# Placing every SBUF tile, and the arena, at a multiple of 256 bytes instead of 128

## The reference

```python
for l in range(DEPTH):                      # DEPTH = 2
    m = silu(c) @ ada_w[l] + ada_b[l]       # shifts, scales and gates
    h = modulate(x, m[0], m[1])
    if l % 2 == 0: y = even_mixer(h, hc, ...)      # SSD scan and HGRN2 scan, with a context of 256 tokens
    else:          y = conformer_conv(h, ...)      # gated product, depthwise conv of 31 taps, product
    x = layer_norm(ALPHA * x + m[2] * y)
    x = layer_norm(ALPHA * x + m[5] * conv_glu_ffn(modulate(x, m[3], m[4])))

def conv_glu_ffn(t, w_up, conv_w, conv_b, w_down, rows, cols):
    v, gate = jnp.split(t @ w_up, 2, axis=-1)      # 1024 -> 2 x 2816
    gate = dwconv2d(gate, conv_w, conv_b, rows, cols)
    return (gelu(gate) * v) @ w_down               # 2816 -> 1024
```

## Time and profile before

| | us |
|---|---|
| median of 3 runs | 2833.45 |
| lowest, highest run | 2827.32, 2833.52 |
| profiled execution, its own time | 2828.01 |
| its span, first to last instruction | 2826.2 |
| PE busy (16080 matmuls) | 2643.6 |
| VectorE busy | 1644.6 |
| ScalarE busy | 1090.9 |
| GpSimd busy | 161.7 |

### The profile page before, as it was taken

One profiled execution on the slowest core, in us unless ns is written; L12 is line 12 of the kernel. 1 busy time (PEld: TensorE's weight loads), 2 busy tenths in 40 slices (PEclk: granted clock), 3 DMA queues, 4 the chain that ended last, 5 costly groups with the idle time before them and its releaser, 6 DMA issues. The chain is left out here.

```text
span 2826.2 us, 41654 instructions
## 1 busy us (share of the span) xinstructions
PE 2643.6 (94%) x16080; PEld 2040.3 (72%) x16080; DVE 1644.6 (58%) x2595; ACT 1090.9 (39%) x1805; POOL 161.7 (6%) x170
## 2 busy tenths in 40 slices
PE   6978899988889999999998999999899998999998
PEld 3753598876668788887664788888588765788876
DVE  3526412257766587853898688853763676544432
ACT  3441211136563455521524455522321254355421
POOL 0005300013213000000000000000000000000000
PEclk9989999999999999999999999999999998999999
DMA  8734312211114133241111233331431000233241
GB/s 306 246 108 145 124 46 60 59 43 40 43 44 131 46 109 91 87 123 47 55 49 34 68 107 94 96 113 52 124 91 45 3 17 28 86 96 96 82 119 61
DMA packets 382116, 240.93 MB, mean 85 GB/s; under 512 B 7825, under 2 KB 353809, under 8 KB 381969
## 3 DMA queue, kind: packets, MB, share of 16 engines
q1 hardware_dynamic: 381968, 238.89, 28.1%
HBM read 236.24 MB, written 2.10 MB: 84 GB/s over the span
## 5 line engine op out<-in xcount | busy, mean ns | idle before, releaser
L1164 DVE SCALAR_TENSOR_TENSOR ffn_acc<-ffn_pad,cols_sb,ffn_acc 128x512 f32<-128x512 f32 x380 | 263.6, 745 | 31.2 <-ACT ffn_acc L1091 31.1
L249 PE MATMUL bank<-ffn_x_high,pre_high 128*128 128x512 f32 x528 | 209.4, 397 | 4.9 <-DVE ffn_x_low L480 3.8
L251 PE MATMUL bank<-ffn_x_high,pre_low 128*128 128x512 f32 x528 | 207.3, 393 | 0.0
L250 PE MATMUL bank<-ffn_x_low,pre_high 128*128 128x512 f32 x528 | 207.3, 393 | 0.0
L251 PE MATMUL bank<-ffn_x_high,ffn_w_low 128*128 128x512 f32 x528 | 205.5, 389 | 0.0
L249 PE MATMUL bank<-ffn_x_high,ffn_w_high 128*128 128x512 f32 x528 | 205.5, 389 | 0.0
L250 PE MATMUL bank<-ffn_x_low,ffn_w_high 128*128 128x512 f32 x528 | 205.4, 389 | 0.0
L249 PE MATMUL bank<-ffn_h_high,ffn_down_w_high 128*128 128x512 f32 x480 | 188.7, 393 | 0.0
L251 PE MATMUL bank<-ffn_h_high,ffn_down_w_low 128*128 128x512 f32 x480 | 187.7, 391 | 0.0
L250 PE MATMUL bank<-ffn_h_low,ffn_down_w_high 128*128 128x512 f32 x480 | 187.6, 391 | 0.0
L754 ACT ACTIVATE ffn_down_w_high<-ffn_down_ring 128x1408 fp32r<-128x1408 f32 (+1 forms) x45 | 60.5, 1344 | 207.1 <-PE bank L251 175.7
(11 more groups left out here) (732 smaller groups left out, 6237.8 us busy)
## 6 DMA issues: line engine op xcount, KB each, us to landing
ada_ring<-in_ada_w SPq DMA_DIRECT2D x48, 1024.0 KB, 7.0
pre_ring<-in_ffn_w_up SPq DMA_DIRECT2D x88, 512.0 KB, 3.7
pre_ring<-in_ffn_w_in SPq DMA_DIRECT2D x44, 512.0 KB, 3.7
ffn_down_ring<-in_ffn_w_down SPq DMA_DIRECT2D x28, 704.0 KB, 4.5
pj_ring<-in_w_in SPq DMA_DIRECT2D x24, 512.0 KB, 3.5
ffn_down_ring<-in_ffn_w_out SPq DMA_DIRECT2D x14, 704.0 KB, 4.4
pre_ring<-in_conf_w SPq DMA_DIRECT2D x18, 512.0 KB, 4.8
f_ring<-in_mix_w_in SPq DMA_DIRECT2D x32, 256.0 KB, 3.2
```

The costliest lines, as they stand in the source:

```text
L249: pe.matmul(bank, weights[0], acts[0], start=start, stop=False)
L250: pe.matmul(bank, weights[0], acts[1], start=False, stop=False)
L251: return pe.matmul(bank, weights[1], acts[0], start=False, stop=stop)
L1164: dve.scalar_tensor_tensor(out=dst, in0=src, scalar=conv_w(2 * i + j, n), in1=dst, op0=ALU.mult, op1=ALU.add).then_inc(tapped[j], 1)
```

## The change

One constant, that every request for a place in SBUF names:

```diff
 ARENA = 28 * 1024
-LINE = 128
+LINE = 256
```

## The result

The changed kernel takes 2812.76 us (median of 6 runs, 2804.01 to 2816.26) against 2830.97 us for the kernel before (6 runs, 2827.32 to 2833.52). The ratio is 0.9933, with a 95% interval of 0.9916 to 0.9950: faster by 14 to 24 us. The forecast was 2818 us, in a range of 2811 to 2827. The profiled execution took 2811.28 us.

The account below looks back on a forecast made before the run. TensorE was taken as the bound in the feed-forward loops, by matmul count times start distance, 5.6 ns dearer for pairs 128 apart. Eight terms summed to 12.8 us; 2830.6 less that gave 2818 us, range 2811 to 2827.

Parts of the forecast that it names:

- Terms 1 to 3: Gains: gate slabs of ffn0 and ffn1 5.4 us; ffn2's down product 2.7; first 16 arena blocks of three down products 0.8.
- Terms 4 and 8: Projections from `pj_w`: 2.1 us gained at 512 tokens, and 0.4 (between 0 and 1.1) where they stream 384 columns.
- Term 5: First projection, `xbc_w`: 288 matmuls no longer 128 apart, 1.1 us gained, between 0 and 1.6.
- Term 6: The second block's first 16 output blocks from the arena: 48 matmuls, 0.3 us gained.
- Term 7: Conformer: 192 matmuls and 48 in its output product, between 0 and 1.3 us; taken as 0, under VectorE's taps.
- VectorE and loads at nothing: Slab splits change at most 8 ns, under PE's work, and ring landing times stay alike; both counted as 0.
- Nothing happens: Rival: distance between starts hangs on something else about the arena, such as its height; 2828 to 2833 us, chance 0.07.
- Half lost: Rival: PE gives time back in other waits, items 3 to 6 go; 2823 to 2827 us, chance 0.14.
- Cheaper loads: Rival: arena loads landing at multiples of 256 get cheaper, some 9 us more at 38 to 170 us; 2809, chance 0.03.
- 256 apart costs: Rival: about 1820 more matmuls 256 apart modulo 512, ffn0's and ffn1's down products first, cost too; up to 2840, chance 0.03.

## Why the prediction was right, and where not

**Cause.** Weights and activations that stand 128 apart modulo 256 cost, in products of 512 and of 384 columns; the place of neither does. Shown from both sides: the arena at 128 is slow by activations at 0 and fast by activations at 128, and the kernel with everything at 128 is as fast as the changed one. The Trainium skill, "SBUF — State Buffer", section "Who interferes with whom", calls TensorE's two read ports independent; the 226.7 against 232.4 ns of these runs speak against it for this pair of reads. What happens inside the chip when the two stand apart, these runs don't show; they show the price by distance.

**Terms 1 to 3** (5.4 + 2.7 + 0.8). The loops gave 2.9 us each and ffn2's down product with its first blocks 2.9, where 2.7, 2.7 and 3.0 stood. The first 48 matmuls of a loop gave nothing, as forecast: in ffn0 they take 14.01 us before (961.88 to 975.89) and 14.00 after (964.88 to 978.88), paced by the activations. The loops' 0.2 us over the forecast lie in the ten later arena blocks, 11.16 to 10.88 us or 5.8 ns a matmul, and in the stack's, 10.89 to 10.88. The first blocks of ffn0 and ffn1 went from 232.6 to 227.7 ns, 0.2 us each; the down products behind them scatter by up to 1 us from trace to trace, so in the whole stretch that doesn't show.

**Terms 4 and 8** (2.1 + 0.4), and **what the sum lacked**. Without the clock's part, the projections gave 5.9 less 3 to 3.5, or 2.4 to 2.9 us, and the pitch of the products of 384 columns went from 178.1 to 175.6 ns, 0.5 us: both terms hold. What failed is the step that a time saved before a stage's waits can only be lost in them; the sum has no term for the clock, which it put at nothing without a reason. With the quicker products, 3 to 3.5 us that half clock had cost in the projections went, and 2.0 to 3.6 us in attention. That, 5 to 7 us, is about what lies between the sum of 12.8 and the gain, 18.2 us by the medians and 20.4 by the ratio of the repeated runs; the gain's interval, 14 to 24 us, is too wide to check it more closely.

**Term 5** (1.1, between 0 and 1.6). The pitch of `xbc_w` went from 232.4 to 227.6 ns, but the stage's time scatters by 2 us and more with its half clock (203.1 before, 205.7 and 201.3 after), so what arrived can't be read. Beside it the same weights go over the context's tokens in 240 matmuls of 256 columns, also 128 apart before, which the count left out. They gave nothing: their pitch is 122.1 to 122.4 ns in the four traces with that distance and 123.1 in the eight with 0. **Term 6**: 233.1 to 227.3 ns and 52.5 to 52.2 us, the 0.3 forecast. **Term 7**: the pitch of the conformer's arena products fell from 232.4 to 228.2 ns and the stage stayed at 196.3 to 196.5, under VectorE's taps, as argued from the earlier trace rows.

**VectorE and loads at nothing**: medians of 1220 and 1225 ns after against 1219 and 1225, and landings at most 0.2 us shorter; both hold, since the gain comes without the shorter landings too, with every tile 128 off.

**The rivals.** Nothing happens: refuted by the pitches. Half lost: nothing came back as waits in the loops, since PE has none there but the first activations. Cheaper loads: refuted by the kernel with every tile 128 off, whose loads land in 4.5 and 4.4 us and whose time is the changed kernel's; and the modulation's weights, which the rival went by, land in 7.0 to 7.4 us before and 7.1 to 7.4 after. The argument against it was too strong, though: the earlier trace rows compared two stages, and within one, ffn2, a ring 128 off costs 4.4 us against 4.2. The Trainium skill, "DMA: Bandwidth & Descriptors", section "How a descriptor splits into AXI transactions", says that a descriptor that doesn't start at a multiple of 256 bytes costs extra beats; these 0.2 us agree with it in direction. 256 apart costs: ffn0's down product reads 226.7 ns at that distance.

**The number.** 2818 was 5 us too high, about the clock's part; the range held it by 1.8 us at its low end. That end came from every term at its full price and the lowest base, rounded down, and not from anything that could give more, so that it held is in part luck: 2 of the 6 runs lie below it.

## What to carry to other kernels

Where TensorE is the bound and takes one pass of 512 columns after another (at 256 columns nothing was to be gained here), place the weight tile and the streamed tile alike modulo 256 bytes (both at 0, or both at 128), and look for the mismatch in the distance between starts, since the duration of a matmul shows 4 ns of the 5.6. Price such an edit per pair, by the matmuls that stand apart before and after: it is worth 2.4% of their time, and a careless shift of one tile can cost as much. In a stage with short pauses of TensorE, trace the kernel before more than once before a few microseconds are put down to an edit or to chance: the granted clock moves by either.

## What was not expected of the hardware

A distance of 32 bytes costs as much as one of 64, 160 or 224, 6.5 ns, and 192 only 2; at 256 columns a distance of 128 costs nothing. A pause of 1.91 us on TensorE is followed by 3.4 us at half clock in one kernel and by none in another with the same instructions, and one tile's address, 128 bytes over, takes 6.0 us from its stage and 3.6 from the next in a pair of runs. In ffn2 a load of 704 KB lands 0.2 us sooner when its ring starts at a multiple of 256; in ffn0 and ffn1 that can't be told from the scatter. Between runs of one kernel the stretch from 610 to 845 us takes 234.6 or 242.7 us, with 19 or 35 us at half clock.
